# Re-tiling the output projection of a hybrid decoder step: 512 + 512 + 32 token columns in place of 3 × 352

## The reference, cut to what matters

```python
h = rms_norm(x, norm1)
proj = jnp.einsum('btd,de->bte', h, w_in)      # branches A and B, and two gates
...
merged = jax.nn.sigmoid(gate_a) * (o_a @ w_br_a) + jax.nn.sigmoid(gate_b) * (o_b @ w_br_b)
x = x + merged @ w_out                         # the output projection and the residual
h2 = rms_norm(x, norm2)
x = x + jnp.square(jax.nn.relu(h2 @ w_up)) @ w_down
return x, new_win, s_new.astype(x.dtype), new_conv
```

## Time and profile before

| | |
|---|---|
| time, median of 3 runs | 2179.8 us (2178.13 to 2181.57) |
| span of the profiled execution, first to last instruction | 2175.8 us |
| TensorE matmul busy / weight load busy | 91% / 88% |
| VectorE, ScalarE, GpSimd busy | 34%, 29%, 26% |
| output projection, from job 0's first matmul to job 7's last transpose | 1301.9 to 1409.8 us |

### The profile page before, as it was taken

One profiled execution on the slowest core, in us unless ns is written; L12 is line 12 of the kernel. 1 busy time (PEld: TensorE's weight loads), 2 busy tenths in 40 slices (PEclk: granted clock), 3 DMA queues, 4 the chain that ended last, 5 costly groups with the idle time before them and its releaser, 6 DMA issues.

```text
span 2175.8 us, 32922 instructions
## 1 busy us (share of the span) xinstructions
PE 1977.4 (91%) x12388; PEld 1913.5 (88%) x12388; DVE 733.8 (34%) x1549; ACT 635.6 (29%) x1390; POOL 564.9 (26%) x334
## 2 busy tenths in 40 slices
PE   5877995997798679999999899999999999999998
PEld 5876895896798679998899899999999999999998
DVE  5523342242243312222221652364135115314513
ACT  7331241332233133333333342322013113202311
POOL 1131122123113011110111353444134214313432
PEclk8898997998998799999999999999999999999999
DMA  4222122122122242344454232311111111111112
GB/s 131 80 75 66 52 95 85 51 77 79 51 90 76 58 134 86 115 130 132 131 150 167 97 126 79 98 40 49 49 49 39 49 49 40 49 49 44 45 59 80
DMA packets 235493, 174.17 MB, mean 80 GB/s; under 512 B 15917, under 2 KB 224890, under 8 KB 235218
## 3 DMA queue, kind: packets, MB, share of 16 engines
q1 hardware_dynamic: 201026, 143.09, 21.7%
q10 hardware_dynamic: 34352, 29.37, 4.0%
HBM read 135.14 MB, written 47.72 MB: 84 GB/s over the span
## 4 chain that ended last, share of the span: by engine, by line
PE 74%; DMA 9%; DVE 8%; ACT 4%; issue 4%; POOL 1%; SPq 0%; ACTq 0%; DVEq 0%; POOLq 0%
PE dense L215 47%; PE dense L240 10%; DMA at_scratch<-at 5%; PE work L1292 2%; PE work L1304 1%; PE work L956 1%; PE work L966 1%; PE work L1342 1%; DVE systems L817 1%; PE work L1325 1%; DVE summed L1644 1%; PE work L1284 1%; PE work L896 1%; DMA sq<-t_scratch 1%; PE work L923 1%
## 5 line engine op out<-in xcount | busy, mean ns | idle before, releaser
L204 POOL TENSOR_TENSOR WL<-Wraw,WH 128x1024 fp32r<-128x1024 f32 (+1 forms) x131 | 312.8, 2388 | 1181.0 <-ACT WH L199 1180.8
L215 PE MATMUL dense<-hH,WH 128*128 128x352 f32 x1464 | 484.0, 331 | 13.7 <-issue 7.4
L215 PE MATMUL dense<-hL,WH 128*128 128x352 f32 x1464 | 477.3, 326 | 0.0
L215 PE MATMUL dense<-hH,WL 128*128 128x352 f32 x1464 | 477.2, 326 | 0.0
L240 PE MATMUL dense<-hH,WH 128*128 128x352 f32 x720 | 267.6, 372 | 61.0 <-ACT fill L249 61.0
L215 PEld LDWEIGHTS dense<-hH,WH 128*128 128x128 f32 x1464 | 281.8, 192 | 16.4 <-issue 11.6
L215 PEld LDWEIGHTS dense<-hL,WH 128*128 128x128 f32 x1464 | 282.3, 193 | 0.0
L215 PEld LDWEIGHTS dense<-hH,WL 128*128 128x128 f32 x1464 | 281.0, 192 | 0.0
L215 PE MATMUL dense<-gH,WH 128*128 128x352 f32 x768 | 248.4, 323 | 4.7 <-issue 2.3
L215 PE MATMUL dense<-gL,WH 128*128 128x352 f32 x768 | 247.7, 323 | 0.0
L215 PE MATMUL dense<-gH,WL 128*128 128x352 f32 x768 | 247.7, 323 | 0.0
(11 more groups left out here) (299 smaller groups left out, 2664.2 us busy)
## 6 DMA issues: line engine op xcount, KB each, us to landing
Wraw<-in_w_in SPq DMA_DIRECT2D x51, 512.0 KB, 4.1
Wraw<-in_w_up SPq DMA_DIRECT2D x32, 512.0 KB, 4.0
Wraw<-in_w_down SPq DMA_DIRECT2D x32, 512.0 KB, 3.5
raw<-qkv_scratch SPq DMA_DIRECT2D x7, 1584.0 KB, 8.3
cache<-in_cache_win SPq DMA_DIRECT2D x20, 512.0 KB, 6.0
qkv_scratch<-fill ACTq DMA_DIRECT2D x54, 176.0 KB, 2.1
gb_scratch<-fill ACTq DMA_DIRECT2D x24, 176.0 KB, 2.1
gates<-ga_scratch SPq DMA_DIRECT2D x8, 528.0 KB, 3.6
```

Of the source, the lines that this page charges most:

```text
L204: G.tensor_tensor(WL[:, s, 0:k], Wraw[:, s, 0:k], WH[:, s, 0:k].bitcast(F32), ALU.subtract).then_inc(sem("w_split"), 1)
L215: ins = PE.matmul(out[:, 0:TN], w[:, s, k0 + k, :], x[:, k, cols], start=(k == 0 and i == 0), stop=(k == nk - 1 and i == 2))
```

## The change

The output projection alone gets tiles of its own, `OUT_CUTS`: columns 0 to 511, 512 to 1023 (together the prompt), and 1024 to 1055 (the samples). A job has 72 matmuls as before: 24 of 512, 24 of 512 and 24 of 32 columns. The total of columns is the same. ScalarE's copies follow the cuts. The prompt's tile 0 now needs the first two of the three 352-column pieces of `hL`, so its last chunk waits for `h_lo` 41 instead of 40, and tiles 1 and 2 for 42.

```diff
-        def product(n0, t, out, xH, xL, k0=0, nk=KD, before_last=None):
+        def product(n0, t, out, xH, xL, k0=0, nk=KD, before_last=None, cut=None):
 
             s = n0 % 2
-            cols = slice(TN * t, TN * t + TN)
+            c, w_ = cut or (TN * t, TN)
+            cols = slice(c, c + w_)
...
-                    ins = PE.matmul(out[:, 0:TN], w[:, s, k0 + k, :], x[:, k, cols],
+                    ins = PE.matmul(out[:, 0:w_], w[:, s, k0 + k, :], x[:, k, cols],
...
+        OUT_CUTS = ((0, 512), (512, 512), (TP, TS))
...
-                    for t in range(NG):
+                    for t, (c, w) in enumerate(OUT_CUTS):
                         done(act, n0 + 2 * i, t)
-                        A.activation(x1[:, bass.ds(o, 1), TN * t:TN * t + TN], dense[t][:, 0:TN].rearrange("p (o t) -> p o t", o=1), ACT.Copy).then_inc(sem(f"d_free{t}"), 1)
+                        A.activation(x1[:, bass.ds(o, 1), c:c + w], dense[t][:, 0:w].rearrange("p (o t) -> p o t", o=1), ACT.Copy).then_inc(sem(f"d_free{t}"), 1)
...
+                    pe.wait_ge(sem("w_split"), n0 + 3 + 2 * i)
                     for t in range(NG):
-                        job(pe, n0, n0 + 2 * i, t, before_last=lambda: pe.wait_ge(sem("h_lo"), 40 + t))
+                        pe.wait_ge(sem(f"d_free{t}"), n0 + 2 * i)
+                        product(n0, t, dense[t], hH, hL, before_last=lambda: pe.wait_ge(sem("h_lo"), 41 + min(t, 1)),
+                                cut=OUT_CUTS[t]).then_inc(sem("d_done"), 1)
```

## The result

The change made the kernel slower: 2200.57 us (median of 4 runs, 2197.65 to 2202.71) against 2178.97 us (4 runs, 2177.88 to 2181.57), a ratio of 1.0096 with an interval of 1.0082 to 1.0109. Predicted were 2198.9 us and a range of 2190 to 2206. Measured a second time beside its variants the ratio was 1.0103 (1.0089 to 1.0117). The profiled execution took 2197.65 us in all, the shortest of the four, and its span is 2195.7 us, 19.9 us over the span of before; the medians are 21.6 us apart.

What follows compares the result with a forecast made beforehand. TensorE, busy 91% of the span, was taken to bound the kernel. The terms 15.1 + 0.4 − 0.3 + 3.9 = +19.1 us on the median of 2179.8 gave 2198.9 us, range 2190 to 2206.

Steps and rivals of the forecast that it cites:

- wider and narrower matmuls, 7 jobs: Output projection on TensorE: three tiles take 570 ns instead of 480 per chunk and product, +15.1 us over seven jobs.
- job 1 at the lower clock: Job 1 still runs its first 6.8 us at the lower clock, losing 3.2 us instead of 2.8: +0.4 us.
- falls of the clock: TensorE's clock falls behind two or three of seven jobs, 1.55 us each: +3.9 us.
- behind job 7: VectorE's adds start earlier after the smaller third copy, where the MLP waits for gL: −0.3 us, once.
- The narrow matmul: A 32-column matmul in the output projection costs its 128 × 128 weight load, 112 ns.
- Rivals 3 and 4: On the narrow matmul: 3, its load hidden, 2177.1 us, 5%; 4, narrow fp32r costs up to 222 ns, 2217.4 us, 4%.
- The wide matmul: A 512-column matmul in the output projection takes 229 ns, between 226 (fixed 13 ns) and 233 (proportional to columns).
- Job 0's growth: Job 0 grows by 2.16 us inside the 3.2 us in which TensorE waits for WL: nothing added.
- rival 2: The clock falls behind every job of the output projection, +10.9 us in place of 3.9: 2205.9 us, chance 15%.
- rival 1: The clock holds through the output projection, so its term is nothing: +15.2 us, 2195.0 us, chance 20%.

Runs made afterwards that it cites:

- load of 32: The change, with the samples' narrow tile loading 128 x 32 weights instead of 128 x 128, 96 of 128 features left out: 2182.32 us.
- loads of 32: Kernel before, cuts of 3 x 352 kept, every output projection matmul loading 128 x 32 weights, 96 of 128 features left out: 2175.24 us.
- pairs: The change, with tile 0 as before, then matmuls of 512 and 32 columns from tiles 1 and 2 taking turns: 2191.81 us.
- halves: The change, with the 24 narrow matmuls split into two runs of 12, half of tile 1 ahead of each: 2190.79 us.
- 464: The change, with output projection tiles cut to 464, 464 and 128 columns: 2184.46 us.
- 400: The change, with output projection tiles cut to 400, 400 and 256 columns: 2178.5 us.

## Why the prediction was right, step by step

The terms, on the spans of the two profiled executions:

| term | predicted | measured | from |
|---|---|---|---|
| wider and narrower matmuls, 7 jobs | +15.1 | +15.8 | 7 × (13.92 − 11.67) |
| job 1 at the lower clock | +0.4 | −0.2 | (16.45 − 13.92) − (14.44 − 11.67) |
| falls of the clock | +3.9 | +6.1 | 1.55 + 1.49 + 1.50 + 1.59 |
| transposes at full clock | 0 | +0.5 | 7 × (1.12 − 1.05) |
| behind job 7 | −0.3 | −0.9 | 1430.93 to 1457.74 against 1409.83 to 1437.52 |
| ahead of job 1, and the rest | 0 | −1.4 | job 0 starts 1.61 earlier, job 1 follows it 0.58 later; −0.3 behind 1457.74 |
| sum | +19.1 | +19.9 | |

The sum came closer than its terms. The eight jobs with all between them grew by 22.7 us (107.9 to 130.6), where the forecast had 19.4 for them; the profiled execution made up for it mostly by an early start of job 0, ahead of which nothing had been changed. The medians, 21.6 us apart, are 2.5 us over the forecast. That the spans came so near is luck.

**The narrow matmul** came at the 112 ns of its nearest row, and the load of 32 shows that the reason was the right one: a quarter of the load's width, 32 ns. Rivals 3 and 4 are out.

**The wide matmul** took 232 ns, where 229 was taken between 226 and 233. The question left open there is settled by four widths: 352 columns take 160 ns, 400 take 182, 464 take 211 and 512 take 232, all 2.2 columns per ns, where a fixed 13 ns would give 180, 206 and 226 for the last three. So the upper end was right. And the reason offered beside it, a share of the weight load, is excluded by the run with loads of 32.

**Job 0's growth was free,** as the step said: the idle time ahead of job 1 is 1.59 us instead of 3.2, again released by WL. It is not the 1 us forecast, as WL itself began 0.6 us later behind the last piece of hL. In the order of time after:

```profile
1316.99 0.79 PE L216 MATMUL dense<-hH,WH 128*128 128x512 f32 x1 [1.59 <-POOL WL L204]
```

**The clock's term was right in kind and too small:** four falls instead of 2.5, each at the price read from the earlier trace rows (1.5 us). The interpolation between runs of 16 and 32 leaned to the lower side for no good reason; eight long runs out of eight had fallen. And most of the falls did not come behind those runs, as the prediction read them, but inside. In the first run of 32, from 1003.66 to 1008.06:

```profile
1003.80:1006.50 2.70, 2.70 (x26) 2.70 (x26) 0.00 (x0) 1.52 (x2) 0.37 (x1) 1.00 0.49 150
1006.60:1008.00 1.40, 1.40 (x9) 1.38 (x8) 0.00 (x0) 0.00 (x0) 1.40 (x1) 0.50 0.01 4
```

The clock fell 2.9 us after this run began, and in the other three runs of 32 after 2.5, 3.0 and 3.5 us. A run of 24 lasts 2.7 us, so the rows spoke for more than two or three falls in seven jobs.

**Job 1's fall** was kept in the sum "as now", and its term came out (−0.2 for +0.4). The reason may not be the one of before. The idle time ahead of job 1 was 1.59 us in the change and 1.39 in its repetition, both with a fall and both directly behind 24 narrow matmuls and the transposes. In the profiles without such a run ahead the clock held with 1.16 us idle (pairs), 1.53 (halves), 2.53 (464) and 3.20 (loads of 32), and fell with 3.21 (before), 3.37 (400) and 3.48 (load of 32). So in the change the narrow run of job 0 probably has its part in this fall too, and without it the term would have been some −2.8. That it came out was partly luck, and no experiment took the two apart.

**What was wrong beside the size is the stretch that I counted.** The prediction joined the narrow matmuls and the transposes to one thin stretch of 3.7 us, and rival 2 leaned on that, with the rule of the Trainium skill ("TensorE: Matmul & The Clock Gate", Part 4: PE-mode transpose) that transposes do not count as busy. With the narrow tile in the middle the falls stay, and with 12 narrow matmuls ahead of the transposes they are gone. So the transposes add nothing that is seen here; whether they count as busy none of the runs can say. Rival 2's time (2205.9) did not come, rival 1's (2195.0) neither: a clock that holds is what the halves and the pairs have, and there it gives 2190.8 and 2191.8, lower than rival 1 said, as the fall ahead of job 1 goes as well.

**Behind job 7** 0.9 us were saved, not 0.3; the last copy of 32 columns is part of it, but GpSimd's adding of the squares was also 0.5 us shorter (2.77 against 3.31 us in the chain of waits). It goes with GpSimd's idle time just ahead of it: 0.8 us in the change, 0.1 before, and 0.36 us in the loads of 32, where it took 3.08. Whether that is the cause was not tested.

## What to carry to other kernels

A tile whose columns take less time than its weight load costs what the load costs: add up max(columns, load) over the tiles before changing a tiling, and keep each tile above it (here 256 columns). With the total of columns fixed, wide tiles give nothing back, as a matmul costs in proportion to its columns. If narrow matmuls can't be avoided, spread them between wide ones, which here gave back 8 of 21 us; and look at the idle gaps of the stage, where moving one load in a queue gave 6.9 us, and no tiling tried here gave any.

## What the runs showed of the hardware that was not expected

- TensorE can show a busy share of 100% and still be given the lower clock: behind 24 matmuls of 32 columns (2.7 us, each bound by its load) it fell to 0.50 for 3.4 us in four to six of the eight jobs (three profiles). Behind 12 it fell in none of 16 runs, and with 128 columns beside each load in none of eight jobs, each in one profile.
- fp32r matmuls run at 2.2 columns per ns at the upper level of the clock, from 352 to 512 columns, with 128 × 128 and with 128 × 32 weights alike; at the lower level 352 columns take 293 ns, which is exactly 1.2 GHz. What holds them back at the upper one is not shown.
- Where the load is the limit, a matmul of 32 columns costs 112 ns with weights 128 wide and 32 ns with weights 32 wide.
- In turns of 512 and 32 columns the starts are 315 and 27 ns apart: single gaps say nothing there, only the pair's 339 ns does.
